# A hybrid GLA and Gated-DeltaNet trunk: operands on 64-byte lines, split and transpose order, scan entry

## The reference, cut to what matters

```python
def gdn_mixer(h, w_in, conv_w, a_log, dt_bias, head_norm, w_out):
    proj = h @ w_in                                   # q, k: 8 x 128 columns, v and z: 8 x 256, beta, a
    qkv, z, beta_logit, a_logit = jnp.split(proj, ...)
    qkv = jax.nn.silu(causal_depthwise_conv(qkv, conv_w))      # four taps along the tokens
    ...
    o = run_segments(gdn_chunk_scan, s0, q, k, v, beta, log_a)  # meta chunk of 16, 16 chunks of 64
    o = rms_norm(o, head_norm) * jax.nn.silu(z)
    return o @ w_out

def gdn_chunk_scan(q, k, v, beta, log_a, s0, c):
    ...
    m = jnp.where(strict, jnp.einsum('bhnid,bhnjd->bhnij', kb, k) * decay_mat, 0.0)
    sol = lax.linalg.triangular_solve(m, rhs, left_side=True, lower=True, unit_diagonal=True)
```

## Time and profile before

| | us |
|---|---|
| median of 3 runs | 1422.35 (1421.91 to 1423.25) |
| the profiled execution | 1421.89 |
| its span, first to last instruction | 1420.1 |
| PE busy in it | 1393.1 (98%), 8242 matmuls |
| DVE busy | 764.3 (54%) |
| ACT busy | 454.9 (32%) |
| POOL busy | 412.1 (29%) |

### The profile page before, as it was taken

One profiled execution on the slowest core, in us unless ns is written; L12 is line 12 of the kernel. 1 busy time (PEld: TensorE's weight loads), 2 busy tenths in 40 slices (PEclk: granted clock), 3 DMA queues, 4 the chain that ended last, 5 costly groups with the idle time before them and its releaser, 6 DMA issues.

```text
span 1420.1 us, 20905 instructions
## 1 busy us (share of the span) xinstructions
PE 1393.1 (98%) x8242; PEld 1175.2 (83%) x8242; DVE 764.3 (54%) x905; ACT 454.9 (32%) x942; POOL 412.1 (29%) x361
## 2 busy tenths in 40 slices
PE   8999999999999999999999999799999999999997
PEld 6878799978888889999999999688876777777776
DVE  5224522134454347656556798999924755444442
ACT  5334621133222244343344533321134522211121
POOL 3213134342111122222222286224242622122200
PEclk9999999999999999999999999999999999999999
DMA  5521344376445135655667355534389866555530
GB/s 195 184 89 46 90 142 150 132 267 199 157 159 185 54 85 120 123 121 120 126 165 166 71 110 91 102 98 127 118 283 250 237 186 179 152 145 149 156 90 30
DMA packets 291100, 200.51 MB, mean 141 GB/s; under 512 B 165018, under 2 KB 254250, under 8 KB 290755
## 3 DMA queue, kind: packets, MB, share of 16 engines
q1 hardware_dynamic: 284418, 187.73, 47.9%
q10 hardware_dynamic: 6592, 11.54, 2.9%
HBM read 131.93 MB, written 67.29 MB: 140 GB/s over the span
## 4 chain that ended last, share of the span: by engine, by line
PE 54%; DVE 6%; issue 1%; ACT 1%; DMA 1%; POOL 0%; ACTq 0%; DVEq 0%; POOLq 0%
PE banks L2175 17%; PE banks L2959 13%; PE banks L2238 12%; DVE gdn L2491 3%; PE banks L3015 2%; PE banks L3048 2%; PE banks L3020 2%; PE banks L3029 1%; PE banks L3003 1%; PE banks L2116 1%; PE banks L2972 1%; DMA gdn_z<-gdn 1%; PE banks L1821 1%; DVE gdn L2502 1%; DVE gdn L1665 1%
## 5 line engine op out<-in xcount | busy, mean ns | idle before, releaser
L2175 PE MATMUL banks<-hn_hi,gdn 128*128 128x352 f32 x1488 | 295.8, 323 | 0.0
L2175 PEld LDWEIGHTS banks<-hn_hi,gdn 128*128 128x128 f32 x1488 | 244.5, 188 | 3.1 <-issue 2.7
L2491 DVE SCALAR_TENSOR_TENSOR gdn<-gdn,conv_taps,gdn 128x1040 f32<-128x1040 f32 x96 | 169.5, 1765 | 28.9 <-ACT gdn L2302 26.1
L2238 PE MATMUL banks<-gdn,hn_hi 128*128 128x512 f32 x512 | 164.1, 400 | 8.5 <-ACT gdn L2288 7.5
L2175 PE MATMUL banks<-hn_lo,gdn 128*128 128x352 f32 x744 | 167.8, 320 | 0.0
L2439 POOL TENSOR_TENSOR gdn<-gdn,gdn 128x1024 fp32r<-128x1024 f32 x31 | 90.3, 2913 | 247.0 <-ACT gdn L2277 247.0
L2175 PEld LDWEIGHTS banks<-hn_lo,gdn 128*128 128x128 f32 x744 | 126.9, 188 | 0.0
L2238 PEld LDWEIGHTS banks<-gdn,hn_hi 128*128 128x128 f32 x512 | 96.7, 190 | 34.4 <-issue 12.2
L920 PE MATMUL banks<-gdn,hn_hi 128*128 128x512 f32 x384 | 120.5, 395 | 0.0
L2238 PE MATMUL banks<-gdn,hn_lo 128*128 128x512 f32 x256 | 101.8, 398 | 0.0
L2959 PE MATMUL banks<-gdn,gdn 128*128 128x512 f32 x384 | 95.5, 398 | 1.4 <-DVE gdn L3174 1.2
(11 more groups left out here) (317 smaller groups left out, 2324.3 us busy)
## 6 DMA issues: line engine op xcount, KB each, us to landing
gdn<-in_gdn_w_in SPq DMA_DIRECT2D x32, 512.0 KB, 4.2
gdn_v<-gdn SPq DMA_DIRECT2D x64, 132.0 KB, 4.0
gdn<-in_x SPq DMA_DIRECT2D x16, 512.0 KB, 4.0
gdn<-in_gla_w_in SPq DMA_DIRECT2D x32, 256.0 KB, 4.2
gdn_kq<-gdn SPq DMA_DIRECT2D x16, 512.0 KB, 4.1
gdn<-in_gdn_w_in SPq DMA_DIRECT2D x32, 256.0 KB, 4.1
gdn<-gdn_kq SPq DMA_DIRECT2D x16, 512.0 KB, 3.7
gdn<-gdn_ek SPq DMA_DIRECT2D x16, 512.0 KB, 5.6
```

The lines of the kernel that those rows point to most:

```text
L2175: return pe.matmul(acc[n % 2][:, b, 0:m], w[n % 2][:, kt, :], x[:, kt, PAD + s:PAD + s + m], start=(kt == 0 and e == 0), stop=(kt == KT - ...
L2238: mm = pe.matmul(z_bank(grp * TT + t), x[:, kt, P + t * P:P + (t + 1) * P], z_half(w, p_), start=(kt == 0 and e == 0), stop=(kt == KT - 1 ...
L2491: dve.scalar_tensor_tensor(cv[:, :], xs[:, tap:tap + L], T.cw[:, tap, t:t + 1], cv[:, :], ALU.mult, ALU.add).then_inc(S("ni_conv"), 1)
```

## The change

It does the following, in one edit:

- `LINE` = 16 floats. `take` puts float32r tensors on multiples of it; `A_DEC` becomes 80; `hn` and the arena get bases that are multiples of 64 bytes, and `hn` is padded by `LINE`, so that both start on a line. `SPANS` becomes 352, 352, 336, starting at tokens 0, 352 and 704.
- `split_lo(n)` for n >= `v_tile(3)` = 20 waits for the convolution of tile n-2.
- DVE transposes v of tile n-2 after the convolution of tile n-1. `PORTION` is 3200, and `invert(..., fine=True)` yields after every one or two operations (752 units with blocks of 8).
- POOL, not DVE, multiplies the meta inverses by beta, at the end of their inversion.
- SP stores the meta inverses early, loads the meta chunk as soon as the inversion is over, stores the inverses of chunks 0 and 1 alone (`gdn_ua_first`, two DMAs of 8 partitions each), loads chunk 0 of those, and only then stores all inverses. Weights' row 4, v and the inverses of chunk 1 are loaded later. `St` and the others are placed so that only ACT's chunk 0 and later loads wait for the large store. DVE no longer waits for it.
- z's last group uses all four slots.
- POOL decays the meta keys before it decays chunk 0.
- `out_project(7)` accumulates in PSUM banks 0 and 1 and does not wait for `out_project(6)` to be read.

```diff
-SPANS = [(0, 352), (352, 344), (696, 344)]
+SPANS = [(0, 352), (352, 352), (704, 336)]
...
-def invert(dve, sem, flat, stride, size, ct, tt, tmp):
+def invert(dve, sem, flat, stride, size, ct, tt, tmp, fine=False):
...
+                if fine:
+                    yield 2 * (n + 120)
+            if not fine:
+                yield 2 * s * (n + 120)
...
-            at = row.end
-            row.end = at + -(-math.prod(shape[1:]) // 8) * 8
+            size = math.prod(shape[1:])
+            unit = LINE if dt == F32R else 8
+            at = -(-row.end // unit) * unit
+            row.end = at + -(-size // 8) * 8
...
-A_DEC = GH * 2 * NT
+A_DEC = -(-GH * 2 * NT // LINE) * LINE
...
-            return k % 4 if k < G3 * TT else 1 + k % 2
+            return k % 4
...
-            sp.wait_ge(S("ni_u"), 4)
+            sp.wait_ge(S("ni_um"), 1)
             sp.dma_start(T.gdn_uam, m_rows).then_inc(S("ni_uam_out"), 16)
+            sp.wait_ge(S("ni_inv"), steps(C))
+        def store_first(sp):
+            sp.wait_ge(S("ni_u"), 2)
+            for c in range(FIRST):
+                sp.dma_start(T.gdn_ua_first[c], sc_x[c::NCH]).then_inc(S("ni_ua_out"), 16)
+        def store_ua(sp):
+            sp.dma_start(T.gdn_ua, sc_x).then_inc(S("ni_ua_out"), 16)
...
+                pool.wait_ge(S("ni_minv"), steps(NMETA))
+                pool.tensor_tensor(m_rows, m_rows, bc(m_g[:, 1, :].rearrange("p (j o) -> p j o", o=1),
+                                                      [NH, NMETA, NMETA]), ALU.mult).then_inc(S("ni_um"), 1)
...
             for n in range(2, NIN):
+                if n >= v_tile(3):
+                    pool.wait_ge(S("ni_conv"), CONV * (nth(n - 2) + 1))
                 split_lo(n)
...
-            PORTION = 3800
+            PORTION = 3200
...
-                if i is not None:
-                    ev_v(i)
                 if n - 1 == GATE:
                     gate_logs()
                 else:
                     conv(n - 1)
+                if i is not None:
+                    ev_v(i)
...
-            sp.wait_ge(S("ni_uam_out"), 16)
             load_meta()
             load_kt(0)
+            F.store_first(sp)
+            sp.wait_ge(S("ni_ua_out"), F.ua_first)
+            load_ua(0)
             load_kt(1)
-            sp.wait_ge(S("ni_ua_out"), 16)
-            load_ua(0)
+            for k in range(F.tiles - 4, F.tiles):
+                F.z_stored(sp, k)
+            F.store_ua(sp)
             load_ek(1)
...
+            sp.wait_ge(S("ni_ua_out"), F.ua_all)
+            F.z_stored(sp, F.tiles)
...
+            load_ua(1)
+            load_v(1)
             sp.wait_ge(S("ni_zdone"), F.tiles + 2)
-            load_rows(2, 3, 4)
+            load_rows(2, 3)
...
-                wait(pe, S("ns_yd"), 2 * t)
+                if t < TT - 1:
+                    wait(pe, S("ns_yd"), 2 * t)
...
-            act.wait_ge(S("ni_ua_out"), 16)
             act.wait_ge(S("ns_mv"), 1)
             act.activation(vn[RM[0], :, :], pK[RM[0], :, :], ACT.Copy).then_inc(S("ns_mvn"), 1)
+            act.wait_ge(S("ni_ua_out"), F.ua_all)
...
-            dve.wait_ge(S("ni_ua_out"), 16)
...
-            base = -(-nc.sbuf_base // 32) * 32
-            sb("hn", [P, 2 * KT * TP + 8], F32, hctx)
+            base = -(-nc.sbuf_base // (4 * LINE)) * 4 * LINE
+            sb("hn", [P, 2 * KT * TP + LINE], F32, hctx)
```

106 lines of the change are left out of this document (56 added, 50 removed).

## The result

The changed kernel takes 1414.24 us (median of 8 runs, 1412.74 to 1419.28), the kernel before 1422.68 in the same jobs: ratio 0.9945, 95% interval 0.9932 to 0.9957. It is faster by 8.4 us, where 21 were forecast, and lies outside the range of 1394 to 1413. The profiled execution took 1412.95 us, its span 1411.1.

What follows compares the result with a forecast made beforehand. PE's matmuls and stalls were taken to bound the kernel; -7.9 - 5.0 - 7.3 + 0.5 + 1.0 - 0.8 - 1.2 = -20.7 us gave 1401.5 us, with a range of 1394 to 1413.

Steps and rivals of the forecast that it cites:

- What bounds the kernel: PE, busy 98%: its matmuls and stalls set the time, other engines matter only where PE waits.
- Pitch, 512 columns: GLA, z and L2959: both operands on 64-byte lines save 4 ns in each of 1964 matmuls, -7.9 us.
- The spans: Tiles' matmul triples of 1040 columns: matched lines save 5 ns in each of 1000, -5.0 us (0 to -10).
- The stall before z: Between tiles and z: stall falls from 7.7 to 2.4 us, 2.0 of slow-clock matmuls go, -7.3 us (0 to -9.7).
- POOL's new wait: Tiles: split_lo waits for the convolution of tile n-2, only tile 25 looks tight, +0.5 us (0 to +3).
- The scan's entry: Start of scan: reordered loads and stores fit narrowly, +1.0 us (0 to +6); four z slots end a PE stall, -0.8.
- The tail: Last projection: out_project(7) with its own banks no longer waits for DVE's reads, -1.2 us.
- The sum: All terms added: -20.7 us, giving a forecast of 1401.5 us.
- The first: Rival on pitch: 64-byte lines do not matter, both pitch terms go, 1414.4 us; chance 0.12.
- The third: Rival at the scan's entry: large store lands at 1066, some 4 us of stall plus slow clock, 1406 us; chance 0.13.

Runs made afterwards that it cites:

- after: The kernel with the whole change, against the kernel before: 1414.24 us, ratio 0.9945.
- The table of shorter matmuls: PE alone, 352, 344 and 336 columns at 36 pairs of operand places, no model computed: 158.3 to 166.7, 153.6 to 159.9, 153.2 to 156.0 ns.
- the order part alone: Kernel before plus POOL's low part and DVE's transposes behind the convolution, smaller pieces, PORTION 3200; old entry, tail, placement: 1424.19 us, ratio 1.0013.
- placement by the right rule: Kernel before plus float32r tensors on 64-byte lines and the arena on a multiple of 256 bytes, spans 352, 344, 344: 1415.66 us, ratio 0.9948.
- the one of all four parts: after plus arena on 256 bytes, spans 352, 344, 344, small stores in 512-byte packets, v of chunk 3 ahead of rows 12 and 13: 1409.92 us.
- the one with v ahead: v of chunk 3 loaded ahead of rows 12 and 13: 1412.20 us on after, 1409.03 on the kernel with the old spans; text names both.
- the old spans: after with the arena on a multiple of 256 bytes and spans 352, 344, 344: 1407.66 us, ratio 0.9900.
- SBUF to SBUF: Kernel with arena on 256 bytes, spans 352, 344, 344 and v of chunk 3 ahead, plus chunk 0's inverses moved without DRAM: 1405.47 us, ratio 0.9885.

## Why the prediction was wrong, point by point

- **What bounds the kernel: right.** PE's stalls were at the places read from the earlier trace rows: the 7.5 us is cut to 1.7, and the 1.2 us is gone. In place of the 0.8 us there are 2.4 now, which belong to the scan's entry below.
- **Pitch, 512 columns, -7.9: wrong, and the step that failed first.** The earlier trace rows compares two pairs of places, 128/64 and 160/64 modulo 256. The step took "both operands on a 64-byte line" for what makes a matmul fast, where "64 bytes apart modulo 256" says the same of these rows. No pair that was on lines and 128 bytes apart had run in the kernel before, and that is the pair which the change makes. L920 and L888 lost what their good half had (232.5 ns throughout), z gained 1 ns, L1303 gained most (128/160 to 192/192, 2.1 us over its stretch), and L2996 some 1 us. Measured for all of placement, this term and the next: 3.9 us alone, 4.6 within after, of 12.9. Of the 12.3 us that are missing from the forecast of 20.7, 8 to 9 are here. The charge of 4 ns a matmul was near what a good pair gives (4 to 7 ns); the pairs that the change makes are not good ones.
- **The spans, -5.0: wrong.** The earlier trace rows was compared with the best rate of another length. The table of shorter matmuls has no such rate, and the tiles took 382.1 us before and after.
- **The stall before z, -7.3: right at its place** (-7.7), though alone worth nothing to the kernel, as under The sum. 2.07 us are left for 2.4, the transpose ends at 896.9 where 898.0 was forecast, and the clock stayed at 1.00.
- **POOL's new wait, +0.5:** PE never waits for L2461, in tile 25 neither, and the tiles are at most 0.2 us longer with the new order than without it (382.35 against 382.14 in the order part alone).
- **The scan's entry, +1.0 - 0.8: wrong by 3 us**, and wrong in its reason. I let a store take 4 us, for which no row stood; the two small ones take 8.5, and they hold up ACT's issues, of which the working did not speak. PE's stalls between 1040 and 1126 us are 4.3 where 1.0 had been, +3.3 against the +0.2 of the sum. A step that was priced only by what waits for it has also a price for what shares its engines. The fourth slot was counted as a gain, -0.8. The wait for a slot at 1047 did go, but with four slots ACT still waited 8.67 us for one where the large store went first: what counts more is when z's stores land. The rest of the entry's forecast held: ACT's first copy of chunk 0 came at 1063.94, right behind its product.
- **The tail, -1.2: right**, 1.3.
- **The sum.** The terms were added as if independent. They are not: the earlier trace rows shows the entry 13 us behind a store, and what PE gains before 1030 can be lost there. The order part alone lost all of its 7.7 us, and placement by the right rule was 10.6 us ahead at z's 500th matmul (first 50 us left out) and lost 5.6 us behind it, in a profile that is the slowest of its five. With the new entry and tail the order part pays: all but placement is worth 4.0. The new entry without the new order was not run.
- **The rivals.** The first, that lines of 64 bytes do not matter, gave 1414.4, within 0.2 us of the result, but by luck: the place does matter, by up to 7 ns a matmul, and what placement gained, some 4 us, was nearly what the entry and the overlap of the terms took back. The third had the entry as the stall, behind the large store; the stall came at 1040 already, beside the small ones.

## What to carry to other kernels

An address effect read from two rows is one distance measured, not a rule: before it is multiplied by 2000 matmuls, the pairs that the change will make must have been seen, and a kernel of TensorE alone maps them in one run. Such a map holds for the length it was made with: that of 512 columns did not hold for 352. Time gained ahead of a fixed transfer is only kept if what stands at that transfer (here an inversion of DVE, a store of 4 MB, and the evictions queued behind it) is moved as well; so a term of the sum is worth its size only up to the next such place. A store from a few partitions is slow by where these partitions lie and by how few they are: the same 512 KB took 6.7, 4.5 and 2.6 us.

## What the runs showed of the hardware that I had not expected

- Float32r matmuls of 512 columns take 227 ns, TensorE working alone, when moving and stationary operand lie at the same place modulo 256 bytes, 229 when the moving one is 64 bytes further, 233 to 234 otherwise. Shorter ones (352, 344, 336 columns) have another pattern and were at no place measured that good a column (0.447 ns at best, against 0.443). Why is open.
- After an idle stretch of PE of 2.4 to 2.5 us the granted clock came out either way. With 2.39 and 2.40 us before z it fell to 0.50 about 1 us into z in two kernels (the one of all four parts, and the one with v ahead), and seven or eight matmuls took 427 ns. With 2.41 and 2.50 us in two others (the old spans, and SBUF to SBUF) it stayed at 1.00. The forecast counted on 2.4 us being safe; the change itself had 2.07.
- Where all inverses are stored first, ACT's DMA of 256 KB, issued at 1036.27, 0.3 us before the store of 4 MB by SP, landed at 1049.97, 0.7 us after that store: another queue was no way round it.

What remains open: why distances 0 and 64 are the good ones, why the first 50 us of the program differ by up to 1.8 us between profiles (matmul 200 starts between 50.8 and 52.6), how much the move from SBUF to SBUF is worth, and whether PE's stall before L3066 at 1120 to 1126, which came and went, follows from the order of SP's loads.
